# Reading a conditioning matrix in thirds: one part ahead of the token chunks, two parts inside them

## What is computed

```python
mod = c @ w_ada + b_ada                       # (9 x 1024) @ (1024 x 6144), fp32, 24 MB of weights
sh1, sc1, g1, sh2, sc2, g2 = jnp.split(mod, 6, axis=-1)
u = x * (1.0 + sc1[:, None]) + sh1[:, None]   # needs sh1, sc1: the first third
proj = u @ w_in
...                                           # pooling mixer, RG-LRU
mix = jnp.concatenate([y_pool, y_lru], axis=-1) @ w_out
x = _layer_norm(ALPHA * x + (1.0 + g1[:, None]) * mix, ln1_g, ln1_b)   # needs g1
u2 = x * (1.0 + sc2[:, None]) + sh2[:, None]                           # needs sh2, sc2
y_moe = _hier_moe(u2, w_group, b_group, w_route, b_route, w_gate, w_up, w_down)
x = _layer_norm(ALPHA * x + (1.0 + g2[:, None]) * y_moe, ln2_g, ln2_b) # needs g2
```

## Time and profile before

| | us |
|---|---|
| median of three runs | 1424.78 (1421.13 to 1426.93) |
| the profiled execution, device time | 1424.33 |
| its span, from the first to the last instruction | 1422.6 |
| head, to the first product of chunk 1 | 164.8 |
| one chunk (the third) | 43.64 |
| PE busy | 1184.7 (83% of the span) |
| DVE busy | 901.3 (63%) |
| TensorE clock granted, mean | 0.914 |

### The profile page before, as it was taken

How to read it: one execution, slowest core, us unless ns; L and a number is a source line. 1 busy time by engine, 2 the same in 40 slices (tenths; PEclk the granted TensorE clock), 3 DMA queues, 4 the chain that set the end, 5 groups by cost and what they waited for, 6 DMA issues and landing times. The chain is left out here.

```text
span 1422.6 us, 23126 instructions
## 1 busy us (share of the span) xinstructions
PE 1184.7 (83%) x6473; PEld 952.0 (67%) x6474; DVE 901.3 (63%) x1824; ACT 535.7 (38%) x915; POOL 545.4 (38%) x545
## 2 busy tenths in 40 slices
PE   6697899999999866799999418999999999999400
PEld 1122699999999765688887317778778787788300
DVE  1114659898899848555655595556676666643398
ACT  0200453535544360222222204445556545533232
POOL 1012022112222043556565243455565455444264
PEclk9897899999999888899999658999999999999755
DMA  8990011011111055244444408888899798654582
GB/s 260 363 349 4 1 38 59 16 43 59 59 59 43 16 183 180 94 147 162 144 162 134 154 15 290 217 216 207 231 268 269 203 269 207 147 111 97 133 310 111
DMA packets 114671, 214.47 MB, mean 151 GB/s; under 512 B 17669, under 2 KB 67337, under 8 KB 114597
## 3 DMA queue, kind: packets, MB, share of 16 engines
q1 hardware_dynamic: 93903, 163.20, 33.5%
q0 software_dynamic: 20736, 50.89, 16.2%
HBM read 153.36 MB, written 85.96 MB: 168 GB/s over the span
## 5 line engine op out<-in xcount | busy, mean ns | idle before, releaser
L1523 PE MATMUL bank<-parts 128*128 128x256 f32 (+2 forms) x1616 | 570.0, 353 | 37.4 <-POOL parts L567 17.5
L1525 PE MATMUL bank<-parts 128*128 128x256 f32 (+2 forms) x1616 | 553.0, 342 | 0.0
L1524 PE MATMUL bank<-parts 128*128 128x256 f32 (+2 forms) x1616 | 552.3, 342 | 0.0
L1523 PEld LDWEIGHTS bank<-parts 128*128 128x128 f32 x1616 | 309.0, 191 | 78.5 <-issue 20.8
L1525 PEld LDWEIGHTS bank<-parts 128*128 128x128 f32 x1616 | 308.4, 191 | 35.6
L1524 PEld LDWEIGHTS bank<-parts 128*128 128x128 f32 x1616 | 309.3, 191 | 31.9
L1470 PE MATMUL bank<-ident,arena 128*128 128x128 f32 (+4 forms) x788 | 118.3, 282 | 26.2 <-DVE arena L1166 8.5
L1470 PEld LDWEIGHTS bank<-ident,arena 128*128 128x128 f32 (+4 forms) x788 | 94.3, 147 | 54.9 <-issue 11.6
L545 POOL TENSOR_TENSOR arena<-arena 128x256 f32<-128x256 f32 (+1 forms) x36 | 26.1, 728 | 270.3 <-DVE h_last L1082 247.5
L1351 DVE TENSOR_TENSOR parts<-arena,parts x90 | 104.8, 1220 | 17.9 <-ACT parts L855 17.9
L880 ACT ACTIVATE arena<-bank,w_now 128x512 f32<-128x512 f32 x96 | 66.1, 689 | 127.3 <-PE bank L1525 73.0
(11 more groups left out here) (258 smaller groups left out, 1544.5 us busy)
## 6 DMA issues: line engine op xcount, KB each, us to landing
ada_arena<-in_w_ada SPq DMA_DIRECT2D x12, 2048.0 KB, 11.0
arena<-in_w_gate SPq DMA_DIRECT2D x16, 1024.0 KB, 5.8
arena<-in_w_up SPq DMA_DIRECT2D x16, 1024.0 KB, 9.4
arena<-in_w_down SPq DMA_DIRECT2D x16, 1024.0 KB, 13.1
arena<-in_x_prompt SPq DMA_DIRECT2D x8, 1024.0 KB, 6.6
yT_d<-arena SPq DMA_DIRECT2D x16, 512.0 KB, 4.4
arena<-yT_d SPq DMA_DIRECT2D x16, 512.0 KB, 4.7
arena<-in_x_prompt SPq DMA_DIRECT2D x16, 512.0 KB, 3.3
```

The lines of the kernel that those rows point to most:

```text
L1523: pe.matmul(out, x_hi, w_hi, start=start, stop=False)
L1524: pe.matmul(out, x_hi, w_lo, start=False, stop=False)
L1525: return pe.matmul(out, x_lo, w_hi, start=False, stop=stop)
```

## The change

The matrix is cut by columns into a first third (2048 columns, `sh1` and `sc1`) and two more of 2048 columns each. The first third is read ahead of everything, in eight blocks of 128 rows (1 MB each, one for each k). The other two thirds are read by slices: slice k is 128 rows of both thirds, 2 x 1 MB. Slice 0 is read and multiplied at the end of the head, slices 1 to 7 in chunks 1 to 7.

The products have another shape: `cT` is padded with zeros to 32 columns, and the four groups of 512 columns go to the four strips of 32 partitions of one bank, so that a bank holds 2048 columns of the result. In a chunk, eight products (two banks, 4 and 5, four strips each) stand ahead of the last projection; they don't accumulate over chunks in PSUM, and DVE adds each bank to `mod_out` (`add_slice`) behind `u_low`, and picks the next chunk's column block of `cT`. In chunk 8, DVE adds the bias, and SP stores `mod_out` to `mod_d` with eight transfers, for which it waits ahead of the loads of `w_out`.

Besides, the small loads of the head move from SP's queue to ACT's; `w_in` is loaded without waiting for products; the sample projection runs with k outermost; and the last norm's loads use six semaphores in turn instead of seventeen, so that SP waits for an earlier load before it issues the sixth one after it. The total count of conditioning products stays at 96.

```diff
-            for n in range(3):
-                sp.dma_start(w_ada[n], ada_d[n]).then_inc(S[f"ada{n}"], 16)
...
+            for k in range(KD):
+                sp.dma_start(w_ada[k], ada_d[k][:, 0:2048]).then_inc(ada_in[k], 16)
...
+            for j in range(4):
+                sp.dma_start(w_in[:, 2 * j:2 * j + 2, :], w_in_d[:, 2 * j:2 * j + 2, :]).then_inc(S[f"w_in{j}"], 16)
...
+            sp.wait_ge(S["ada_mm"], KD)
+            sp.dma_start(w_ada0, ada_d[0][:, 2048:6144].rearrange("p (b n) -> p b n", b=2)).then_inc(S["ada0_in"], 16)
...
+            with sp.Fori(1, NCH - 1) as i:
                 load_x(i + 1)
+                for b in range(2):
+                    sp.wait_ge(S["slice_mm"], 2 * i + 1 + b)
+                    load_slice(i + 1, b)
                 store_y(i)
...
             sp.wait_ge(S["out_evac"], 3)
+            sp.wait_ge(S["mod_stored"], 16 * 8)
             load_out((2, 3, 4, 7))
...
+            def ada_slice(c, w, out):
+
+                for j in range(4):
+                    last = pe.matmul(out[32 * j:32 * j + 32, :], c, w[:, 512 * j:512 * j + 512], start=True, stop=True)
+                last.then_inc(S["slice_mm"], 1)
...
+            def mixers(i, turn_next, slices=False, after_slices=None):
                 for order in range(3 * NG):
+                    if slices and order == 3 * NG - 1:
+                        pe.wait_ge(S["cT_picked"], i)
+                        pe.wait_ge(S["gates_evac"], 2 * NG * i + 6)
+                        for b in range(2):
+                            pe.wait_ge(S[f"ada_in{b}"], 16 * i)
+                            ada_slice(cT_now[:], w_ada_next[b], bank[4 + b])
+                    if order == 2 * NG and after_slices is not None:
+                        pe.wait_ge(S["slice_ok"], after_slices)
...
                 if not last:
                     u_low(i + 1)
+                    for b in range(2):
+                        add_slice(2 * i + b, b, bank[4 + b])
+                    dve.wait_ge(S["slice_ok"], 2 * i + 2)
+                    pick_cT(i + 1)
...
+            dve.wait_ge(S["slice_mm"], 2)
+            o.did(dve.tensor_scalar(mod_out[0:64, 0, :], bank[1][0:64, :], 1.0, None, ALU.add))
+            o.step(dve.tensor_copy(mod_out[64:P, 0, :], bank[1][64:P, :]))
+            dve.tensor_scalar(mod_out[:, 1, :], bank[0][:, :], 1.0, None, ALU.add).then_inc(S["slice_ok"], 2)
```

More of the change, by code:

```diff
@@ L150, in build @@
         row_d, row_e = at(18600, DH), at(18056, DH)
-        w_ada = [place(ada_arena, 10240 + n * 4096, KD, 512) for n in range(3)]
-        mod = place(ada_arena, 22528, 6 * D)
+        w_ada = [place(ada_arena, 12288 + k * 2048, 2048) for k in range(KD)]
+        w_ada0 = place(ada_arena, 24576, 2, 2048)
+        w_ada_next = [at(2048, 2048), at(5184, 2048)]
+        mod_in = at(3072, 512)
+        mod_out = at(8768, 2, 512)
+        b_out = at(2048, 2, 512)
         c_rows = at(0, D)
@@ L1485, in _ @@
             pe.wait_ge(S["cT_ok"], 1)
-            def ada(j, first=False):
-                for n in range(3):
-                    if first and n == 2:
-                        turn_vectors()
-                    pe.wait_ge(S[f"ada{n}"], 16 * (j + 1))
-                    if not first:
-                        pe.wait_ge(S["ada_ok"], 3 * j + n - 2)
-                    for k in range(KD):
-                        last = pe.matmul(bank[n][0:NM, :], cT[:, k, :], w_ada[n][:, k, :], start=k == 0, stop=k == KD - 1)
-                    last.then_inc(S["ada_mm"], 1)
-            ada(0, first=True)
-            with pe.Fori(1, 4) as j:
-                ada(j)
+            for k in range(KD):
+                if k == 4:
+                    turn_vectors()
+                pe.wait_ge(ada_in[k], 16)
+                for j in range(4):
+                    last = pe.matmul(bank[0][32 * j:32 * j + 32, :], cT[:, k, :], w_ada[k][:, 512 * j:512 * j + 512],
+                                     start=k == 0, stop=k == KD - 1)
+                last.then_inc(S["ada_mm"], 1)
+            def ada_slice(c, w, out):
+                for j in range(4):
+                    last = pe.matmul(out[32 * j:32 * j + 32, :], c, w[:, 512 * j:512 * j + 512], start=True, stop=True)
+                last.then_inc(S["slice_mm"], 1)
             pe.wait_ge(S["mod_ok"], 1)
-            for k in range(2 * KD):
-                last = turn(bank[6][:, k * NM:(k + 1) * NM], mod[0:NM, k * P:(k + 1) * P], NM)
+            for i in range(4):
+                last = turn(bank[6][:, i * P:(i + 1) * P], mod_in[:, i * P:(i + 1) * P], P)
             last.then_inc(S["modT_mm"], 1)
@@ L1584, in _ @@
             pe.wait_ge(S["uTs_ready"], 1)
-            for n in range(3):
-                cols = slice(DH, 2 * DH) if n == 0 else slice(0, DH) if n == 1 else slice(2 * DH, 3 * DH)
-                for k in range(KD):
+            for k in range(KD):
+                if k % 2 == 0:
+                    pe.wait_ge(S[f"w_in{k // 2}"], 16)
+                for n in range(3):
+                    cols = slice(DH, 2 * DH) if n == 0 else slice(0, DH) if n == 1 else slice(2 * DH, 3 * DH)
                     last = pe.matmul(bank[2 + n][0:NS + 1, :], uTs[:, k, :], w_in[:, k, cols], start=k == 0, stop=k == KD - 1)
-                last.then_inc(S["rows_mm"], 1)
+                    if k == KD - 1:
+                        last.then_inc(S["rows_mm"], 1)
             for n in range(3):
@@ L1605, in _ @@
             with pe.Fori(1, NCH) as i:
-                mixers(i, lambda: turn_chunk(i + 1))
+                mixers(i, lambda: turn_chunk(i + 1), slices=True, after_slices=2 * i)
             def state_rows(n, src, rows):
```

123 lines of the change are left out of this document (72 added, 51 removed).

## The result

| kernel | us, median (lowest to highest) | ratio to before, 95% interval |
|---|---|---|
| before | 1424.04 (1421.13 to 1426.93) | |
| after | 1367.7 (1367.3 to 1375.88) | 0.9626 [0.9606, 0.9647] |

The account below looks back on a forecast made before the run. Weight reads plus a serial chain bound the head, PE the chunks, late `w_out` the passage. Terms -77.9 + 28.0 + 6.0 = -43.9 from 1422.6 gave span 1378.7, time 1380; range 1358 to 1411.

Parts of the forecast that it names:

- the chunks: Chunks 1 to 7: eight slice products ahead of the last projection cost 4.0 us a chunk, 28.0 in seven.
- the passage: Into the output projection: `mod_d` stores delay the `w_out` loads 5.5 us; with DVE's 0.4 in chunk 7, 6.0.
- the head: Start to first split product: shorter conditioning loads bring it from 164.8 to 86.9, a gain of 77.9 us.
- 13.4 - 4.9 = 8.5: Head, last product to sample projection: 13.4 us before, less two DVE additions of 3.67 and 1.22 leaving the path.
- 21.6: Head, projection's end to first split product: 14.7 us as before, plus 1.0 ACT copies, 4.0 slice 0, 1.9 DVE copies.
- pairs: Slice products: strips overlap only by neighbours, n products take n + 1 slots of 0.417 us; chance 0.45, time 1380.
- all four strips at once: Rival: the engine passes a waiting strip's instruction; chunks cost 7 x 1.9 = 13.4 us, time 1362; chance 0.25.
- serial: Rival of no overlap: a chunk's 16 instructions run one after another, 6.9 us a chunk, time 1409; chance 0.25.
- The 2.38: Skill's speedup for three column strips of 512 columns; a chunk's pair would cost 2.8 + 0.25, seven chunks 21 us.
- DVE's added work: Chunks: two adds and a copy behind `u_low`, where DVE waits 1.20 us for ACT, so 0.4 of 1.6 shows.
- All of it shows: Passage: ACT already waits for `w_out`, so the whole 5.5 us delay of SP's loads lengthens the kernel.
- The final loads: End, last norm's loads: keeping six in flight costs 0, with 1 us as the upper bound.

Follow-up runs that it names:

- pool_later: Changed kernel plus one wait: POOL starts its low parts of `w_in` only after DVE has finished the sample tokens' modulation; 1367.38 us, ratio 0.9616.
- bank_inner: Changed kernel with a chunk's eight slice products reordered: strip 0 of both banks, then strip 1 of both, and so on; 1369.1 us, ratio 0.9624.
- no_slices: Changed kernel without slices 1 to 7 (loads, products, additions and copies); slice 0, bias and stores stay; 1349.49 us, ratio 0.9478.
- the second set: The changed kernel executed five times more, with nothing edited; median 1372.39 us, ratio 0.9655.

## Why the prediction was right, and where it was wrong

The time lies inside its range partly by luck. Against the forecast span of 1378.7 the profiled one of 1374.0 has the chunks 13.4 us cheaper, the passage 3.0 and the head 1.5, and a stage longer by 12.8 that was not in the sum.

**The head: right in sum (-79.4 for -77.9), by errors that cancel.** The last products ended 2.6 us earlier than forecast: 1.0 because four strips ran at once, the rest because the loads landed earlier. The step from there to the projection had been put at 13.4 - 4.9 = 8.5 and took 12.9. It priced DVE's operations by how long they took in the kernel before, without asking what runs beside them now: POOL's `w_in_lo` begins at 36.12, released by ACT's split of `w_in`, and DVE's copy at 36.53. That is what it was short: in `pool_later` the step takes 7.4 (from 32.15 to 39.57), so the collision costs 5.5, and the 8.5 without it was 1.1 too much. A sign stood in the rows of before. Of the two DVE operations of one shape in the earlier trace rows, one took 3.67 and the other 1.22, and the long one ended at 117.59, 1.07 us behind the last piece of POOL's `w_in_lo`, as the additions of the tiles do:

```profile
106.35 10.17 POOL L531 TENSOR_TENSOR parts<-arena,parts 128x1536 fp32r<-128x1536 f32 x3 [3.40 <-PE bank L1497]
```

So half of the 4.9 that left the path looks like such a wait; no run tested this place. From the projection's end to the first split product 21.6 were forecast and 18.7 taken; 2.1 of that are slice 0 at 1.92 instead of 4.0.

**The chunks: the mechanism was wrong.** The forecast's "pairs", 4.0 a chunk, rested on the sentence that an instruction whose strip is busy holds up those behind it. It does not (`bank_inner`). The rival "all four strips at once" is what happened: 1.9 forecast, 2.0 to 2.3 measured; serial, 6.9 forecast, 7.3 measured (51.0 against 43.7). The rows of before could not decide it; only the price of each case was to be had from them, and the two that were run came within 0.4. The Trainium skill (TensorEngine Tiling (Array Packing), Theoretical Speedup) gives up to four times for 32 columns; the runs show 3.8. The 2.38 that the prediction quoted is for three strips, which no run here has, and the program order that it quoted with it does not fit `bank_inner`, where four instructions start within 40 ns though the list begins with four of one strip. The prediction let DVE's added work show only in chunk 7, with 0.4; PE's wait of 0.37 a turn for `u_low` shows in each chunk, and makes up most of what a chunk's 2.26 has beyond the 1.85; how much of it the slices cause is not shown.

**The passage: the delay was right, its effect half.** SP's first load was 5.9 us later than before, for 5.5 forecast. "All of it shows" was the step that failed: the wait for the state stores' landing lay behind it and became 1.3 shorter, SP issued the first loads and the state stores 1.1 faster, and the last four loads landed 0.5 faster, so some 3 showed.

**The final loads: right.** SP takes 15.51 us to issue them instead of 8.77, and the stretch is as long as it was.

```profile
1294.19 15.51 SPq L506 DMA_DIRECT2D arena<-z_d  x16
```

**What was not in the sum: the tiles' stage.** The parts that the change acts on give -79.4 + 17.5 = -61.9, which is the sum of the rival "all four strips" to the digit, by luck: its head gains 1.9 too much, its chunks are 1.2 too cheap and its passage 3.0 too dear. In the profiled execution the longer stage is the rest, from -61.9 to -48.6. The stage is longer where DVE's operations stand behind POOL's, and the residual additions alone don't lengthen it: `no_slices` had five long ones and one long product, and 280.3 us; the eight other profiles of changed versions without the tiles' wait had four to six and four or five, and 284.0 to 293.1. With the additions put in order the two stages are alike (278.3 and 277.8). What sets which of the two engines comes first in a tile, and why the changed kernel draws more of these collisions than the kernel before, is not shown.

For the medians this account does not close. That rival's 1362 was missed by 6, and by 10 in the second set, but with the two stages alike the medians are still 55.9 apart and not 61.9. What makes up that difference stays open.

## What to carry to other kernels

Where a product needs few output columns, put several beside each other in column strips; the price here was that of one strip's list, in both orders that were run. When an edit makes two engines work at the same time, ask which operations of VectorE take all their operands from SBUF while GpSimd runs (a copy and a two-operand addition were held here, an addition that read PSUM was not): their old durations no longer hold, and one wait that sets the order can be worth more than the overlap. A delay in a queue counts only as far as no wait behind it takes it up.

## What was not expected of the hardware

Four column strips of 32 with fp32 products ran 16 instructions of 512 columns in 1.85 us against 6.98 in one strip, in either order of the list. A collision of VectorE and GpSimd made a copy of 0.17 us last 3.06, an addition of 0.69 last 3.28, one of 1.23 last 3.50, and a product of 1.23 last 3.25; a stage in which it may or may not happen took 280 to 293 us in the profiles without the extra wait, and 278 to 280 with it.
